# A bisection shared by ScalarE and VectorE: which engine updates the trial, in which slots a step stands, and where the last rows are scaled

## What is computed

```python
iscore = jnp.where(key_pos < limit, iscore, -jnp.inf)
_, sel = lax.top_k(iscore, topk)             # topk = 256 of up to 2048 keys, for every query
...
x = x + concatenate([o_a, o_b]) @ w_out      # o_a: attention over the chosen keys
h = rms_norm(x, norm_ffn_g)
x = x + jnp.square(jax.nn.relu(h @ w_ff1)) @ w_ff2
return rms_norm(x, norm_final_g)
```

## Time and profile before

| | us |
|---|---|
| time, median of 3 runs | 3700.47 (3698.0 to 3703.13) |
| the profiled execution | 3703.72 |
| its span | 3701.8 |
| TensorE busy | 3314.6 (90%) |
| VectorE busy | 2162.4 (58%) |
| ScalarE busy | 2157.3 (58%) |
| GpSimd busy | 1342.0 (36%) |
| count over all columns, m_junk, line 1919 | 401.4 in 248 |
| GpSimd's part of the weights, m_wl, line 1862 | 704.7 in 284 |

### The profile page before, as it was taken

The page is one execution under the profiler, slowest core; times in us unless marked ns, Lnnn a source line. Parts: engine busy times, 40 slices in busy tenths (PEclk is TensorE's granted clock), DMA queues, the critical chain, the costliest instruction groups (busy, mean ns, idle before and its releaser), DMA issues.

```text
span 3701.8 us, 47211 instructions
## 1 busy us (share of the span) xinstructions
PE 3314.6 (90%) x16674; PEld 2741.7 (74%) x16674; DVE 2162.4 (58%) x3720; ACT 2157.3 (58%) x3713; POOL 1342.0 (36%) x709
## 2 busy tenths in 40 slices
PE   6999878888898996888999789999889999989998
PEld 4888757777777785767777567878667878868886
DVE  6344038687977756745646575757575575443223
ACT  4222138577755654597696959696867944433232
POOL 0211053434345434333433233433233333334443
PEclk9999989999999997999999899999999999999999
DMA  3612253423433447423333333334423333342232
GB/s 118 239 58 84 89 121 75 125 70 70 118 97 80 98 135 201 147 83 107 115 100 114 117 98 101 122 93 135 125 90 113 105 110 96 99 127 91 97 97 80
DMA packets 286441, 401.73 MB, mean 109 GB/s; under 512 B 23024, under 2 KB 204400, under 8 KB 281584
## 3 DMA queue, kind: packets, MB, share of 16 engines
q1 hardware_dynamic: 281456, 367.26, 33.7%
q10 hardware_dynamic: 4752, 31.46, 2.3%
HBM read 322.71 MB, written 75.92 MB: 108 GB/s over the span
## 4 chain that ended last, share of the span: by engine, by line
PE 28%; ACT 16%; DVE 9%; issue 5%; POOL 2%; DMA 1%; SPq 0%; ACTq 0%; DVEq 0%; POOLq 0%
PE m_ps L2226 8%; PE m_ps L2228 8%; PE m_ps L2227 8%; ACT m_junk L1919 7%; ACT m_wh L1982 2%; PE m_ps L2349 2%; PE m_ps L2329 2%; ACT m_prob L2009 1%; ACT m_verdict L1921 1%; POOL m_wl L1862 1%; ACT m_trial L1925 1%; DVE m_rl L2064 1%; ACT m_phi L1998 1%; DMA out_dram<-m_tmp 1%; PE m_ps L2314 1%
## 5 line engine op out<-in xcount | busy, mean ns | idle before, releaser
L1862 POOL TENSOR_TENSOR m_wl<-m_raw,m_wh 128x1024 fp32r<-128x1024 f32 x284 | 704.7, 2482 | 1338.4 <-ACT m_wh L1982 1338.3
L2226 PE MATMUL m_ps<-m_ah,m_wh 128*128 128x512 f32 x1280 | 530.9, 415 | 24.9 <-DVE m_acc L2039 9.8
L2228 PE MATMUL m_ps<-m_ah,m_wl 128*128 128x512 f32 x1280 | 511.7, 400 | 0.0
L2227 PE MATMUL m_ps<-m_al,m_wh 128*128 128x512 f32 x1280 | 510.6, 399 | 0.0
L2226 PE MATMUL m_ps<-m_th,m_wh 128*128 128x512 f32 x1024 | 416.8, 407 | 14.8 <-DVE m_tl L2066 11.1
L1919 ACT ACTIVATE m_junk<-m_sc,m_trial 128x1152 int8<-128x1152 f32 (+7 forms) x248 | 401.4, 1619 | 8.0 <-DVE m_sc L2186 7.0
L2228 PE MATMUL m_ps<-m_th,m_wl 128*128 128x512 f32 x1024 | 404.7, 395 | 0.0
L2227 PE MATMUL m_ps<-m_tl,m_wh 128*128 128x512 f32 x1024 | 403.9, 394 | 0.0
L1982 ACT ACTIVATE m_wh<-m_raw 128x1024 fp32r<-128x1024 f32 x284 | 298.3, 1052 | 145.5 <-PE m_ps L2228 130.6
L2064 DVE TENSOR_TENSOR m_rl<-m_rl 128x512 f32<-128x512 f32 x128 | 105.9, 827 | 374.9 <-ACT m_th L1939 374.2
L2226 PEld LDWEIGHTS m_ps<-m_ah,m_wh 128*128 128x128 f32 x1280 | 248.6, 194 | 77.7 <-issue 13.4
(11 more groups left out here) (329 smaller groups left out, 7457.4 us busy)
## 6 DMA issues: line engine op xcount, KB each, us to landing
m_raw<-w_units SPq DMA_DIRECT2D x284, 512.0 KB, 3.5
m_vals<-valsT SPq DMA_DIRECT2D x240, 128.0 KB, 2.4
p_raw<-w_proj SPq DMA_DIRECT2D x72, 256.0 KB, 4.1
m_rot<-rowsQ SPq DMA_DIRECT2D x50, 256.0 KB, 4.2
projT<-work ACTq DMA_DIRECT2D x12, 1024.0 KB, 4.5
g_qkvz<-projT SPq DMA_DIRECT2D x16, 768.0 KB, 5.8
wraw<-w_proj SPq DMA_DIRECT2D x21, 512.0 KB, 4.9
i_rot<-projT SPq DMA_DIRECT2D x32, 256.0 KB, 5.0
```

Of the source, the lines that this page charges most:

```text
L1862: nc.gpsimd.tensor_tensor(wl[:, n % 3, :], raw[:, n % 2, :], wh[:, n % 3, :].bitcast(fp32), ALU.subtract).then_inc(w_lo, 1)
L2226: nc.tensor.matmul(dst, hi, rh, start=first, stop=False)
L2227: nc.tensor.matmul(dst, hi, r_low, start=False, stop=False)
L2228: return nc.tensor.matmul(dst, lo, rh, start=False, stop=last)
```

## The change

ScalarE's probe keeps only the count. Its verdict and the change of the trial become a step of VectorE, `step`: a compare of m_balance with m_goal times the bit, and an operation that takes the or with half a bit and the exclusive or with the trial. The step stands in the slot after its probe, behind `ff_low`; where two probes share a slot (17 pairs) it stands at the end of VectorE's slot, as a `select`. The next probe waits for the step, the step for the probe. The slots from base-6 to base of blocks 1, 2 and 3 hold no step of a search; the rest of the slots up to the same end take all of them. In the last block `out` writes the scaled rows over m_acc in place of m_tmp, and waits for no store.

```diff
@@ OverlapPlan.search
         stop = self.begins(4 * self.NT - 5) - 12
-        total, at = sum(weight(j) for j in self.late), 2.0
+        ends = {x for b in range(1, self.NB) for x in range(self.base[b] - KC + 2, self.base[b] + 1)}
+        free = [x for x in range(2, stop + 1) if x not in ends]
+        total, at = sum(weight(j) for j in self.late), 0.0
...
-                slot = int(at + 1 + i * (span - 3) / len(steps))
+            slots = [free[int(at + 1 + i * (span - 3) / len(steps))] for i in range(len(steps))]
+            for i, (what, slot) in enumerate(zip(steps, slots)):
                 if what == "probe":
                     self.put("act", slot, "probe", n, BITS - 1 - (i - 2))
+                    if slots[i + 1] == slot:
+                        self.put("dve", slot, "select", n, "step", BITS - 1 - (i - 2))
+                    else:
+                        self.put("dve", slot + 1, "step", n, "step", BITS - 1 - (i - 2))
@@ probe (ScalarE)
                 if bit == BITS - 1:
                     act.wait_ge(begun, n + 1)
-                turns.do(nc.scalar.activation(verdict[:, :], balance[:, :], ACT.Sign, scale=-1.0, bias=goal[:, :]))
...
-                    turns.do(nc.scalar.activation(half, verdict[:, :], ACT.Identity, scale=float(2 ** (bit % 16 - 1)), bias=half))
                 else:
...
+                    act.wait_ge(stepped, BITS * n + BITS - 1 - bit)
+                nc.scalar.activation(junk[:, 0:N], sc[:, 0:N], ACT.Sign, scale=-1.0,
+                                     bias=trial[:, :].bitcast(fp32), accum_out=balance[:, :]).then_inc(probed, 1)
@@ select (VectorE)
+                elif what == "step":
+                    dve.wait_ge(probed, BITS * n + BITS - bit)
+                    pick.do(nc.vector.tensor_scalar(step_up[:, :], balance[:, :], goal[:, :], float(2 ** bit), ALU.is_ge, ALU.mult))
+                    nc.vector.scalar_tensor_tensor(out=trial[:, :], in0=step_up[:, :], scalar=2 ** bit // 2, in1=trial[:, :],
+                                                   op0=ALU.bitwise_or, op1=ALU.bitwise_xor).then_inc(stepped, 1)
@@ out (VectorE) and out_store (SyncE)
+        out_row = lambda b, k: tmp[:, k % 2, :] if b + 1 < NB else acc[:, k, :]
...
-                if k >= 2:
+                if b + 1 == NB:
+                    pass
+                elif k >= 2:
                     dve.wait_ge(o_stored[k % 2], 16 * (KC // 2 * b + k // 2))
```

More of the change, by code:

```diff
@@ L1389 @@
         "act": "relu square low values_hi high split exp round mix_high h_high probe root".split(),
-        "dve": "x_add y_add sum_squares ff_low finish mask values_low lower rinv cos prep_low mix_low norm out lead_add select".split(),
+        "dve": "x_add y_add sum_squares ff_low step finish mask values_low lower rinv cos prep_low mix_low norm out lead_add select".split(),
         "pe": "product spread scores values transpose dense squares".split(),
@@ L1546, in search @@
         stop = self.begins(4 * self.NT - 5) - 12
-        total, at = sum(weight(j) for j in self.late), 2.0
+        ends = {x for b in range(1, self.NB) for x in range(self.base[b] - KC + 2, self.base[b] + 1)}
+        free = [x for x in range(2, stop + 1) if x not in ends]
+        total, at = sum(weight(j) for j in self.late), 0.0
         for n, j in enumerate(self.late):
-            span = (stop - 2) * weight(j) / total
-            self.put("sp", int(at) - 1, "score_in", n)
+            span = (len(free) - 3) * weight(j) / total
+            self.put("sp", free[int(at)] - 1, "score_in", n)
             steps = self.SEARCH
-            for i, what in enumerate(steps):
-                slot = int(at + 1 + i * (span - 3) / len(steps))
+            slots = [free[int(at + 1 + i * (span - 3) / len(steps))] for i in range(len(steps))]
+            for i, (what, slot) in enumerate(zip(steps, slots)):
                 if what == "probe":
                     self.put("act", slot, "probe", n, BITS - 1 - (i - 2))
+                    if slots[i + 1] == slot:
+                        self.put("dve", slot, "select", n, "step", BITS - 1 - (i - 2))
+                    else:
+                        self.put("dve", slot + 1, "step", n, "step", BITS - 1 - (i - 2))
                 else:
@@ L1912, in _ @@
             nc.scalar.preload_act_table_set("natural_log_exp_and_others")
-            turns = Steps(act, probed)
             def probe(n, bit):
@@ L1918, in probe @@
                     act.wait_ge(begun, n + 1)
-                turns.do(nc.scalar.activation(junk[:, 0:N], sc[:, 0:N], ACT.Sign, scale=-1.0,
-                                              bias=trial[:, :].bitcast(fp32), accum_out=balance[:, :]))
-                turns.do(nc.scalar.activation(verdict[:, :], balance[:, :], ACT.Sign, scale=-1.0, bias=goal[:, :]))
-                halves = trial[:, :].bitcast(u16)
-                half = halves[:, bit // 16:bit // 16 + 1]
-                if bit % 16:
-                    turns.do(nc.scalar.activation(half, verdict[:, :], ACT.Identity, scale=float(2 ** (bit % 16 - 1)), bias=half))
-                else:
[L1927 to L1930, removed]
+                else:
+                    act.wait_ge(stepped, BITS * n + BITS - 1 - bit)
+                nc.scalar.activation(junk[:, 0:N], sc[:, 0:N], ACT.Sign, scale=-1.0,
+                                     bias=trial[:, :].bitcast(fp32), accum_out=balance[:, :]).then_inc(probed, 1)
             def relu(b, j):
@@ L2092, in out @@
                     dve.wait_ge(al_done, split_at(b, 2 * KC - 2 + k) + 1)
-                nc.vector.scalar_tensor_tensor(out=tmp[:, k % 2, :], in0=acc[:, k, :], scalar=gl[:, k:k + 1],
+                nc.vector.scalar_tensor_tensor(out=out_row(b, k), in0=acc[:, k, :], scalar=gl[:, k:k + 1],
                                                in1=rstd[:, :], op0=ALU.mult, op1=ALU.mult).then_inc(out_done, 1)
@@ L2170, in _, with select @@
             pick = Steps(dve, sel_s)
-            def select(n, what):
+            def select(n, what, bit=None):
                 j = plan.late[n]
@@ L2212, in select @@
                     nc.vector.tensor_scalar(t, t, MASK_BIAS, None, ALU.mult).then_inc(picked, 1)
-            does = {"select": select, "prep_low": prep_low, "x_add": x_add, "sum_squares": sum_squares, "y_add": y_add, "ff_low": ff_low, "norm": norm, "out": out, "mix_low": mix_low, "lead_add": lead_add,
+            does = {"select": select, "step": select, "prep_low": prep_low, "x_add": x_add, "sum_squares": sum_squares, "y_add": y_add, "ff_low": ff_low, "norm": norm, "out": out, "mix_low": mix_low, "lead_add": lead_add,
                     "finish": finish, "mask": mask, "values_low": values_low, "lower": lower, "rinv": invert, "cos": by_cosine}
```

8 lines of the change are left out of this document (4 added, 4 removed).

## The result

The changed kernel takes 3712.4 us (median of 6 runs, 3708.1 to 3719.6); the kernel before took 3700.4 in the same session. The ratio is 1.0035, 95% interval 1.0025 to 1.0045: 12 us slower, small but clear of noise, where I had forecast 3697 with a range of 3685 to 3712. The profiled execution took 3712.1 for a span of 3710.3.

What follows compares the result with a forecast made beforehand. Probes were taken to fill ScalarE until TensorE now and then waits behind one, not to bound the kernel by themselves. Terms +17 - 15 - 1 - 4.7 = -3.7 took the median from 3700.5 to 3697 us, range 3685 to 3712.

Steps and rivals of the forecast that it cites:

- step on VectorE, plain stretches and search 0: Stalled updates on VectorE lose +17 us in plain stretches; in search 0 shorter waits give -1.
- ends of blocks: Last slots of blocks 0 and 1, freed of probes, shorten TensorE's waits: -15 us.
- last rows: Last eight output rows, scaled in place, no longer wait for stores: -4.7 us.
- Six probes go from there: I take 6 us of that: End of block 1: freed of probes, TensorE's 6.6 us wait for the sum of squares loses 6 us.
- is on the path by itself: ScalarE's 166 us relief: none on the path by itself; only small waits in W2 stretches go, some 3 us.
- the stall and the wait behind it: Relu slots of W1 stretches: updates stalled behind GpSimd make ScalarE lag; with clock, together +20 us.
- slot-by-slot count: Pair of slots in a W1 stretch: 9.5 us after the change, 1.7 us behind TensorE, 1.3 us of lag free.
- The race: Update against GpSimd's split behind ff_low: of 48 places the update loses in 44 and wins in 4.
- the two margins that I had named: GpSimd starts before the update by 0.1 us with one high ahead of the split, 0.6 without.
- the signs I had named: Trace signs: long updates, ScalarE idle 2 us in relu slots, near none elsewhere, m_plo waits about as now, gapless last rows.
- Relief wins: Rival: update beats GpSimd or its stall is absorbed, so ScalarE's relief shortens the kernel by 55 us to 3645; chance 0.17.
- The lock decides: Rival: ScalarE sets the pace throughout W1 stretches, nothing caught up; 3745, range from 3712, middle 3729; chance 0.35.

Runs made afterwards that it cites:

- e_noends: The changed kernel with the searches' steps allowed in the ends of blocks again: 3708.5 us, ratio 1.0025 to the kernel before.
- e_tail: The kernel before, probes wholly on ScalarE, with only the last output rows scaled in place: 3692.8 us, ratio 0.9980.
- e_relief: e_tail with ScalarE's verdict and update left out, nothing in their place, the count compared with a constant: 3610.1 us, ratio 0.9756 to the kernel before.
- e_first: The changed kernel with step ahead of ff_low in VectorE's slot, the update keeping two SBUF inputs: 3625.1 us, ratio 0.9803 to the kernel before.
- e_ends_tail: The kernel before, probes wholly on ScalarE, with slots at the ends of blocks left free and last rows in place: 3713.7 us, ratio 1.0040.
- e_dummy2: e_ends_tail with the step's two operations added on VectorE, the second with two SBUF inputs, nobody waiting: 3730.0 us, ratio 1.0085 to the kernel before.
- e_free: The changed kernel with the update as a tensor-scalar operation with one SBUF input: 3629.3 us, ratio 0.9813 to the kernel before.

## Why the prediction was wrong

By its own terms, with the medians:

| term | forecast | measured |
|---|---|---|
| step on VectorE, plain stretches and search 0 | +17 - 1 | +15.7 (e_noends less e_tail) |
| ends of blocks | -15 | +3.9 (the changed kernel less e_noends) |
| last rows | -4.7 | -7.0 (e_tail less the kernel before) |
| sum | -3.7 | +12.6 |

The first measured term includes the small shifts of probes named above. The changed kernel beside the kernel before gives +12.1.

**The step that failed** is the one on the ends of blocks: "Six probes go from there: I take 6 us of that". Two things are wrong in it. The 6.6 us wait for m_sqsum hangs on the probes by 1.3 us only: with them left out it is 5.3, since where m_al waits behind GpSimd's split the chain m_al, m_acc, m_sqsum takes 5.5 us with probes and without. Of the other items at block 1, the 2.7 us off the wait for m_tl came as 0.4 (4.7 to 4.3 in the changed kernel), and the 2 us off that for m_acc as 1.3 (2.1 to 0.8, in the changed kernel and without the probes). At block 0 the wait for m_acc, from which I took 3.5 us, is 3.6 before, 4.5 without the probes and 3.4 in the changed kernel. Leaving out all 13 probes gives 3.3 us by the medians. And the probes don't "go": they stand in plain stretches, where each costs 1.9 us. The prediction charged nothing for that, though its first paragraph had ScalarE 93% busy there. Of the selection steps that move I said "no reason for either sign"; for probes there was one, since 13 more of them then stand in the stretches where ScalarE is short of time.

**What the plain stretches' +16 was made of.** The total was right and its parts were not. I wrote that none of the relief "is on the path by itself" and gave it 3 us in W2 stretches; e_relief has 83. I gave the stall and the wait behind it some 20; e_noends less e_relief is 98. Two errors of about 80 us with opposite signs met in a good sum, and that was luck. The slot-by-slot count (a pair of slots at 9.5 us; measured 9.4 in search 5, relu to relu) was right, but I let the lag be caught up in between at no cost, and took "no relief left" for "relief worth nothing".

**What held.** The race: 42 stalled updates in relu slots where I had counted 44. In 19 of them GpSimd was ahead by 0.1 us, in 4 by 0.18, in 19 by 0.3 to 0.8, mostly 0.58: the two margins that I had named. By the Trainium skill, "SBUF — State Buffer", section "SBUF: two separate sides", an exclusive lock lasts for a whole instruction of whichever engine starts first; the longest update, 2.351 us against 2.39 for GpSimd's split, agrees, and so do e_first and the two updates of the changed kernel that began 0.07 us ahead of the split. The wait for m_tl at the end of block 0 grew, as said, but by 4.3 us (4.8 to 9.1), not 2.5. The last rows lost their gaps. Of the signs I had named, ScalarE's idle time ahead of the count came in the relu slots as said (over 90 us), but some 45 us more came elsewhere, where I had said near none, and the waits for m_plo were not "as large as now" but half as large again (41.1 to 62.6).

**The rivals.** "Relief wins" named the right mechanism for a kernel without the stall, but at 3645, ends and last rows included; without the lock it is 3629, and without the lock and the ends' cost 3611 to 3619. "The lock decides" took in the measured time, its range being from 3712; yet its sign-post, waits for m_plo over 70 us, was not reached (62.6), and it too booked 21 us of gain from ends and last rows.

**What stays open.** Why the free ends cost 21 us beside ScalarE's own update and only about 4 beside the stalling one. A likely reason is that fewer counts then wait for a stall there, but no run separates it. In the traces of e_ends_tail and of the changed kernel some 12 us are lost against e_tail while search 7 runs, and next to nothing in e_noends; which of its steps does it was not tried.

## What to carry to other kernels

Before an operation goes to VectorE, count its SBUF tensor inputs and see what GpSimd does at that moment: in this kernel, with two, it took on the rest of GpSimd's instruction (up to 2.2 us more for a column), with one, or 0.07 us ahead of GpSimd, it cost its 0.2 us, and most of the price was paid by what waited behind it (67 to 76 of 83 us, on another engine). A step taken off one stretch must be priced in the stretch where it lands, and the gain where it left checked against the dependent chain there: leaving it out entirely is the quickest test. And relief of an engine that is nearly full can be worth much even when TensorE waits for it only "now and then" (here 83 us for 166); if a forecast says it is worth nothing, measure it with the work left out.

## What the runs showed of the hardware

- In the changed kernel the 92 updates (one column, two SBUF tensors) that took over 0.3 us all began during an instruction of GpSimd, 79 during a split of weights and 13 during its shorter work on m_rot and m_qlo, and ended 0.01 to 0.03 us behind it. The other 156 took at most 0.3 us.
- A tensor-scalar operation of VectorE on one column with one SBUF tensor and a per-partition scalar did not stall in any of 232 cases (216 to 220 ns), also when it started inside GpSimd's 2.4 us; the same place with two tensors gave 99 of 248 over 0.3 us, 65 of them over 1.5 us, when nobody waited for it (e_dummy2).
- TensorE's granted clock, mean from 1520 to 3020, is 0.95 of 2.4 GHz in the kernel before and after, with 143 and 160 us of TensorE idle; it is 0.98 in e_free with 102 us idle and 0.97 in e_relief with 89.
